# Opening of a two-layer encoder kernel: first input half on ScalarE's queue, first weights on SyncE's; the fifth unit split between the squares, the first pre-norm sum behind it

## The reference, cut to what matters

```python
def swiglu(x, w_gate, w_up, w_down):
    return (jax.nn.silu(x @ w_gate) * (x @ w_up)) @ w_down
...
def reference(x, norm_gains, ffn1_gate, ffn1_up, ffn1_down, ...):
    h = x                                   # (1, 512, 1024) float32
    for l in range(DEPTH):                  # 2 layers
        g = norm_gains[l]
        h = h + 0.5 * rms_norm(swiglu(rms_norm(h, g[0]), ffn1_gate[l], ffn1_up[l], ffn1_down[l]), g[1])
        m = hybrid_mixer(rms_norm(h, g[2]), w_in[l], ...)
        h = h + rms_norm(m, g[3])
        h = h + 0.5 * rms_norm(swiglu(rms_norm(h, g[4]), ffn2_gate[l], ffn2_up[l], ffn2_down[l]), g[5])
    return h
```

## Time and profile before

| | |
|---|---|
| device time, three executions | 1898.43, 1895.52 and 1893.75 us (median 1895.52) |
| profiled execution, first to last instruction (span) | 1894.6 us; its own time around the span is not listed |
| busy shares of the span | PE 99%, PEld 81%, DVE 52%, ACT 37%, POOL 11% |
| mean granted TensorE clock | 0.996 of full speed |
| PE waits in the first 60 us, over 1 us | 2.4, 1.8, 1.5, 1.2 and 1.2 us |

### The profile page before, as it was taken

One profiled execution on the slowest core, in us unless ns is written; L12 is line 12 of the kernel. 1 busy time (PEld: TensorE's weight loads), 2 busy tenths in 40 slices (PEclk: granted clock), 3 DMA queues, 4 the chain that ended last, 5 costly groups with the idle time before them and its releaser, 6 DMA issues.

```text
span 1894.6 us, 25239 instructions
## 1 busy us (share of the span) xinstructions
PE 1867.2 (99%) x9472; PEld 1542.8 (81%) x9472; DVE 987.8 (52%) x1350; ACT 709.2 (37%) x1112; POOL 202.4 (11%) x420
## 2 busy tenths in 40 slices
PE   8999999999999999999999999999999999999998
PEld 6888888887778888888888888889876788888887
DVE  5564442387667544432376544324877574444323
ACT  5333332254654333232253323223656453333321
POOL 2741000013100000000047010000131000000000
PEclk9999999999999999999999999999999999999999
DMA  6334333243213333333333443333512323333331
GB/s 179 105 113 130 93 117 100 81 138 106 66 56 89 91 98 100 96 115 94 93 110 90 143 103 99 109 104 99 159 39 67 98 65 94 100 99 103 106 92 44
DMA packets 330957, 188.61 MB, mean 100 GB/s; under 512 B 6996, under 2 KB 325432, under 8 KB 329848
## 3 DMA queue, kind: packets, MB, share of 16 engines
q1 hardware_dynamic: 324008, 168.13, 30.8%
q0 software_dynamic: 5824, 18.79, 3.4%
q10 hardware_dynamic: 1040, 0.52, 0.1%
HBM read 175.72 MB, written 11.67 MB: 99 GB/s over the span
## 4 chain that ended last, share of the span: by engine, by line
PE 92%; DVE 4%; ACT 3%; issue 1%; DMA 0%; DVEq 0%; ACTq 0%
PE ps L590 18%; PE ps L592 18%; PE ps L591 18%; PE ps L791 8%; PE ps L790 8%; PE ps L792 8%; PE ps L646 1%; PE ps L648 1%; PE ps L653 1%; PE ps L976 1%; PE ps L750 1%; PE ps L749 1%; PE ps L751 1%; PE ps L620 1%; PE ps L631 1%; PE ps L622 1%
## 5 line engine op out<-in xcount | busy, mean ns | idle before, releaser
L1648 DVE TENSOR_TENSOR wl<-raw,wh 128x1024 fp32r<-128x1024 f32 (+1 forms) x260 | 344.9, 1327 | 738.1 <-ACT wh L1157 737.2
L590 PE MATMUL ps<-xh,wh 128*128 128x512 f32 x1536 | 607.2, 395 | 9.7 <-ACT u L1499 6.3
L592 PE MATMUL ps<-xh,wl 128*128 128x512 f32 x1536 | 599.7, 390 | 0.0
L591 PE MATMUL ps<-xl,wh 128*128 128x512 f32 x1536 | 599.3, 390 | 0.0
L1157 ACT ACTIVATE wh<-raw 128x1024 fp32r<-128x1024 f32 (+1 forms) x260 | 295.9, 1139 | 636.3 <-PE ps L792 324.6
L590 PEld LDWEIGHTS ps<-xh,wh 128*128 128x128 f32 x1536 | 289.0, 188 | 74.7 <-ACT u L1499 6.8
L592 PEld LDWEIGHTS ps<-xh,wl 128*128 128x128 f32 x1536 | 289.1, 188 | 60.9
L591 PEld LDWEIGHTS ps<-xl,wh 128*128 128x128 f32 x1536 | 289.3, 188 | 60.0 <-issue 1.7
L790 PE MATMUL ps<-Hh,wh 128*128 128x512 f32 x638 | 248.4, 389 | 0.0
L792 PE MATMUL ps<-Hh,wl 128*128 128x512 f32 x638 | 248.2, 389 | 0.0
L791 PE MATMUL ps<-Hl,wh 128*128 128x512 f32 x638 | 248.2, 389 | 0.0
(11 more groups left out here) (382 smaller groups left out, 2031.6 us busy)
## 6 DMA issues: line engine op xcount, KB each, us to landing
raw<-in_ffn_up SPq DMA_DIRECT2D x88, 512.0 KB, 3.8
raw<-in_ffn_down SPq DMA_DIRECT2D x64, 704.0 KB, 4.6
raw<-in_ffn_gate SPq DMA_DIRECT2D x87, 512.0 KB, 3.8
raw<-in_w_in SPq DMA_DIRECT2D x28, 512.0 KB, 4.0
raw<-in_w_out SPq DMA_DIRECT2D x16, 512.0 KB, 3.7
xrow<-in_x SPq DMA_DIRECT2D x2, 1024.0 KB, 8.6
ssm_t<-evict POOLq DMA_DIRECT2D x8, 256.0 KB, 3.2
ssm_v<-evict POOLq DMA_DIRECT2D x8, 256.0 KB, 2.7
```

What stands on the lines that cost most here:

```text
L590: pe.matmul(bank, w_tile(True, slot, kw), xh[:, kx, :], start=first, stop=False)
L591: pe.matmul(bank, w_tile(True, slot, kw), xl[:, kx, :], start=False, stop=False)
L592: return pe.matmul(bank, w_tile(False, slot, kw), xh[:, kx, :], start=False, stop=last)
L1648: V.tensor_tensor(w_low(slot, k0, nk), raw[:, slot4, 0:nk - k0, :], w_high(slot, k0, nk).bitcast(F32), ALU.subtract).then_inc(w_split, 1)
```

## The change

The first half of x is issued on ScalarE's queue and the first weight unit on SyncE's, behind the gains and the unit matrix. In the first stage the split of unit 4 moves between squares 5 and 6 on ScalarE, its low part between the sums of squares 5 and 6 on VectorE, and the pre-norm sum on TensorE moves from behind the first four units to behind unit 4, where it stands in all other stages.

```diff
-            def x_half(i):
-                sp.dma_start(x_rows[:, :, i, :],
-                             x[0].rearrange("(t p) d -> p t d", p=P)[:, :, i * SEQ:(i + 1) * SEQ]).then_inc(s_in2[i], 16)
-
-            x_half(0)
+            def x_second():
+                sp.dma_start(x_rows[:, :, 1, :],
+                             x[0].rearrange("(t p) d -> p t d", p=P)[:, :, SEQ:2 * SEQ]).then_inc(s_in2[1], 16)
+
             sp.dma_start(par[0:96, 0, 0:P], norm_gains.rearrange("l g (k p) -> (l g k) p", p=P)).then_inc(s_in, 16)
             sp.dma_start(ident[:, :], const[:, K_ID:K_ID + P]).then_inc(s_in, 16)
...
                     for i in range(4):
                         if i == 2:
-                            x_half(1)
-                        if i:
-                            load(i, i, raw[:, i, 0:KD, :], columns((gate, up)[i % 2], l, slice(i // 2 * P, i // 2 * P + P)))
+                            x_second()
+                        load(i, i, raw[:, i, 0:KD, :], columns((gate, up)[i % 2], l, slice(i // 2 * P, i // 2 * P + P)))
                     late_params()
...
                                 mm.then_inc(unit_done, cols[u][2])
-                if s == 0:
-                    pre_norm(s)
-
             def pre_norm(s):
...
-                    if u == 4 and l * 3 + pi:
+                    if u == 4:
                         pre_norm(l * 3 + pi)
...
-            act.dma_start(raw[:, 0, 0:KD, :], ffn1_gate[0:1, :, 0:P].rearrange("a (k p) f -> p (a k) f", p=P)).then_inc(landed[0], 16)
+            act.dma_start(xrow[:, :, :].rearrange("p (t a) n -> p t a n", t=TOK)[:, :, 0, :],
+                          x[0].rearrange("(t p) d -> p t d", p=P)[:, :, 0:SEQ]).then_inc(s_in2[0], 16)
...
-                split_ahead(s, n_first(s))
+                if s:
+                    split_ahead(s, n_first(s))
...
-            for d in range(4, KD):
+            for d in range(4, 6):
+                square_in(0, d)
+            split_ahead(0, n_first(0))
+            for d in range(6, KD):
                 square_in(0, d)
...
-                low_ahead(s, 4)
                 if s:
+                    low_ahead(s, 4)
                     pre_sum(s)
...
-            pre_sum(0, 4, KD)
+            pre_sum(0, 4, 6)
+            low_ahead(0, 4)
+            pre_sum(0, 6, KD)
```

## The result

The changed kernel took 1905.86 us, the median of 5 runs (1902.96 to 1907.85), beside 1898.43 us for the kernel before on the same chip (5 runs, 1893.75 to 1899.0), 7.4 us more. The medians' quotient is 1.0039, the estimated ratio 1.0046 with a 95% interval from 1.0035 to 1.0057. It is slower by more than the 0.3% that a measurement of this kernel can tell. Run again beside other kernels it took 1903.27 us over 1896.21, ratio 1.0037 [1.0024, 1.0049]. The forecast was 1901.0 us, the range 1897.5 to 1903.5.

The account below looks back on a forecast made before the run. TensorE, busy 1867.2 of 1894.6 us, was taken to bound the kernel. Opening -0.4, wait before unit 5 +3.7 and clock +2.2 made +5.5 on 1895.5: 1901.0 us, range 1897.5 to 1903.5.

Parts of the forecast that it names:

- The opening, -0.4: Start to unit 2: swapped loads leave unit 2's landing unmoved, so only its 0.45 us of slack is won, -0.4 us.
- The Trainium skill's rule: Opening, rival: issuers share the same DMA engines, so the opening gives exactly 0; +5.9 us, 1901.4, chance 0.12.
- The wait for unit 4 goes: Before unit 4: its low part ends near 37.95, ahead of TensorE at 39.22, so the 1.16 us wait goes.
- The wait before unit 5, +3.7: Behind the pre-norm sum: unit 5's split waits behind the root, TensorE idles 5.1 us, unit 5 starts 3.7 us later.
- The clock, +2.2, at most 2.8: Behind the idle stretch before unit 5: granted clock near 0.50 slows products, +2.2 us, between 0 and 2.8.
- The base: Whole kernel: the median of the runs before the change, 1895.5 us, to which the forecast added its terms.
- The longer low clock, with nothing from the opening (+6.5): Behind the gap, rival: clock low for 6.1 us or more, opening gives 0; +6.5 us, 1902.0, chance 0.18.
- the change does only what its words say: Unit 4 and opening, rival: the 1.2 us wait and 0.4 us go, nothing else; -1.6 us, 1893.9, chance 0.03.

Follow-up runs that it names:

- queues_only: The kernel before with the two loads swapped between the queues and nothing else; 1896.53 us, ratio 1.0000.
- busy_stall: The changed kernel with 22 idle products on TensorE behind the pre-norm sum, to fill its wait before unit 5; 1900.07 us, ratio 1.0022.
- split5_ahead: The changed kernel with unit 5's split and low part ahead of the root; 1899.44 us, ratio 1.0014.
- split56_ahead: The changed kernel with the splits and low parts of units 5 and 6 ahead of the root; 1895.53 us, ratio .9996.
- busy_delay: The kernel before with 24 idle products on TensorE behind unit 4, a delay without idle time; 1902.51 us, ratio 1.0033.
- gap_changed: The changed kernel with ScalarE's copy of the state's output ahead of a unit's split in both mixers; 1899.13 us, ratio 1.0013.
- changed_again: The changed kernel timed once more with no edit; 1903.27 us, ratio 1.0037.
- second_part_only: The kernel before with unit 4's split and low part between the squares and the sum behind unit 4, loads as before; 1903.28 us, ratio 1.0038.
- gap_before: The kernel before with ScalarE's copy of the state's output ahead of a unit's split in both mixers; 1892.04 us, ratio .9974.
- gap_split56: The changed kernel with units 5 and 6 split ahead of the root and ScalarE's copy ahead of a split in both mixers; 1890.12 us, ratio .9963.

## Why the prediction was wrong, step by step

- **The opening, -0.4:** small, as forecast, but not in the way of the step. In the profile of the result it is -0.23 us. Unit 2 lands 0.24 us earlier, where the step took its landing as unmoved, and its low part, done at 17.82, is still 0.45 us early at 18.27: units 0 and 1 came earlier, and all behind them with it. That profile is the lucky one: in the seven others with the new loads TensorE is done with the first four units 0.2 to 1.4 us later than in before, with a low clock of 6.8 us in the opening instead of 3.4. The runs show neither gain nor loss (queues_only, 1.0000, to 1.7 us). The Trainium skill's rule, *DMA: Bandwidth & Descriptors*, "Issuing engines are not separate DMA queues", that a second issuer saves issue time alone, gave 0: the runs agree with it (1.0000), and can't tell it from 0.4.
- **The wait for unit 4 goes:** right, and unit 4 starts at 38.97 with its low part done at 37.57.
- **The wait before unit 5, +3.7:** right in place and size. It lasts 5.07 us against 5.1; unit 5 is 3.27 us later with the opening counted, 3.5 counted from the end of the first four units (11.53 us instead of 8.01), and 3.5 was measured with the clock held up (busy_stall). Its cause is the order behind the root, shown by split5_ahead and split56_ahead.
- **The clock, +2.2, at most 2.8: the step that failed.** Its mechanism was right: behind the wait the clock is at 0.50, and with the wait filled it is not. Its size was not: the term measured some 3.5 us. In the four profiles with the wait unit 5 takes 7.75 to 8.33 us instead of 5.58, so the stretch right behind the wait costs 2.2 to 2.8, as the step had it. But the changed order has 8.6 to 11.7 us more low clock in a run, 3.4 to 4.2 us at 0.36 to 0.39, and busy_stall leaves 3.5 for it. The step priced one stretch and put all others at nothing, as they were in one profile of before. They are not fixed: by this sum some 1 us of the loss stands in other stretches.
- **The base.** Of the 4.9 us between the forecast and 1905.86, the change's loss makes 1.9 (7.4 instead of 5.5) and the base 2.9: beside the changed kernel, five runs of before had a median of 1898.43, not the 1895.5 of three runs that the forecast stood on. The 1895.5 is also some 0.9 us below what 23 or more runs gave (1896.2 to 1896.6). With +3.3 to 3.5 for the wait and +3.5 for the clock on that, 1903.3 follows, which is what the repetition measured (no test of the 3.5 for the clock, which was taken from it). The first five runs, at 1905.86, lie 2.6 us above it, as those of before beside them lie 2.2 above 1896.21, with mean clocks of 0.990 to 0.993 where the repetition had 0.9925.
- **The rivals.** The longer low clock, with nothing from the opening (+6.5), is nearest to what happened. That the change does only what its words say fell with the wait.

What stays open is where the low clock beyond that behind the wait comes from in the changed order. Being later by itself adds little (busy_delay), and the mixers' waits do not seem to be needed for it (gap_changed, within its interval). Compared product by product with before, the profiles name three places: the opening (+1.4 us in changed_again, +0.5 in second_part_only), the narrow products near 160 us (+1.6 in changed_again) and the first mixer (+1.2 in the profile of the result, +1.1 in second_part_only). Steps of the same size stand at the same places in profiles without the long wait (+0.6 in the opening and +1.1 in the first mixer of queues_only, +1.6 at the narrow products of gap_before). One profile of a kernel can't tell which of them the change lengthens; the narrow products are a candidate that was not tried.

## What to carry to other kernels

When an operation moves behind the work that used to cover its consumers, follow everything that is queued behind that consumer: here the sum moved for a 1.2 us wait, and a split that stood behind its root came 3.3 us later. Price an idle stretch of TensorE by the low clock that follows too, and take that from many runs, not from one profile: here it about doubled the cost. A wait of a few us with low clock behind it is worth looking for on its own: two of them, shortened by moving one instruction on ScalarE, gave 4.3 us.

## What the runs showed of the hardware

**The clock explains most of the spread between runs.** Beside the last three kernels, runs of before at a mean granted clock of 0.997 took 1893.7 to 1895.0 us, at 0.994 1896.8 to 1898.9. Over all runs of before, the low clock accounts for 78 to 91% of the variance in each of the three groups.

**How much idle time the low clock follows is not sharp.** Behind waits of 5.07 us it came in all four profiles that have one. Behind 2.45 us before unit 6 there was none, behind the six waits of 2.2 us in the profiles of the gap kernels three times none (both mixers of gap_before, the second of gap_changed) and three times 3.4 us of it. The waits differ in more than length: ahead of those in the mixers TensorE does narrow products (128 columns and less), ahead of units 5 and 6 full ones, and no run separates the two. One with the low clock, in gap_split56, behind its first mixer's wait:

```profile
469.20:472.60 3.40, 2.84 (x7) 2.29 (x8) 3.30 (x7) 1.45 (x3) 3.40 (x8) 0.54 0.03 4
```

**It also comes without idle time.** In gap_before 32 narrow products stand between full ones with no gap, and the products behind them are slow:

```profile
152.72 0.39 PE L592 MATMUL ps<-xh,wl 128*128 128x512 f32 x1
152.95 4.08 PE L706 MATMUL ps<-cblk,bbd 128*128 128x32 f32 x32
156.84 0.77 PE L590 MATMUL ps<-xh,wh 128*128 128x512 f32 x1
157.42 0.63 PE L591 MATMUL ps<-xl,wh 128*128 128x512 f32 x1
```

They come 0.43 us apart instead of 0.23. The kernel before has the same products there and a clock of 1.00 in its profile; seven of the thirteen profiles have the low clock at this place, six do not, and the changed kernel's own two differ.

**Two queues do not always share.** Queues of the changed kernel from 3 to 5.25 us, packets, MB and time, where both have transfers issued and unfinished:

```profile
q10 hardware_dynamic: 435, 0.89, 102.9%
q1 hardware_dynamic: 7, 0.00, 0.4%
```

ScalarE's queue with the input (2 KB packets) had the engines almost to itself, and unit 0 on SyncE's queue hardly moved. queues_only and changed_again have 436 packets against 2 and 9 in the same stretch. Before, with the input on SyncE's queue, packets were shared evenly. The Trainium skill, *DMA: Bandwidth & Descriptors*, "Queues, rings and completion order", says that each engine takes turns between queues by the packet; the rows of before agree. These do not, unless SyncE's queue had nothing ready to send in that time, which no run decides. In this profile it cost nothing, since unit 2 landed no later than before.
